# Output projection: the residual rows' loads moved behind the loads of the attention's rows

## The chip, the cores and the metric

One core of one Trainium2 chip. The metric is device time in microseconds (us) of one launch. The engines are TensorE (PE; its weight loads are PEld), VectorE (DVE), ScalarE (ACT), GpSimd (POOL) and SyncE (SP), which here issues every DMA.

## The reference, cut to what matters

Two layers on x (1024 rows, 1024 features). The first mixes windowed attention and a two-way gated delta rule, and projects both back onto the residual:

```python
def first_block(x, ...):
    h = x
    xn = _rmsnorm(h, norm_mix_w[l])
    proj = xn @ w_in[l]
    ...
    attn = _windowed_gqa(q_a, k_a, v_a, band_bias, in_window, attn_sink[l])
    gdn = _gdn_mixer(qkv_g, z_g, a_g, b_g, ...)
    h = h + jnp.concatenate([attn, gdn], axis=-1) @ w_out[l]
    hn = _rmsnorm(h, norm_ffn_w[l])
    h = h + jnp.square(jax.nn.relu(hn @ w_ffn_in[l])) @ w_ffn_out[l]
```

The change bears on the line with `w_out`, and there on how `h` (the residual, the input x) reaches the core's memory. A second layer follows (pooling, convolution and stick-breaking attention, gates, projection); the change doesn't name it.

## The kernel before, in words

Data lies feature-major: 8 row blocks of 128 features by 1024 positions, in two halves of 512 (half 0 and half 1). Every large product is made of three passes over operands split into a high and a low part: high weight by high data (line 631), low weight by high data (633), high weight by low data (635). A product of the output projection, stage P3, is one output block m for one half: 8 row blocks, so 24 matmuls. TensorE takes the products in a fixed order: (m 0, half 1), (1, 1), (0, 0), (1, 0), then m 2 to 4 with both halves each (half 0 first), then m 5 to 7 of half 0, then of half 1.

**Operands of P3.** Row blocks 0 to 3 are the attention's output. Attention runs over 8 blocks of 128 positions; after block n VectorE takes it from its bank (`ao`, line 1648) and, for n under 7, SyncE stores it to DRAM (`aout`, "outgoing rows"). `ya(h, j)` loads row block j of half h back ("the attention's rows"): for half 1 once `aout(6)` is complete, for half 0 once `yah(1, j)` and `yal(1, j)` have read its buffer. `yah` (ScalarE, line 997) makes the high part and `yal` (VectorE, line 1425) the low part. Row blocks 4 to 7 are the delta rule's output: `zl(h, j)` loads gate rows, `zm` (VectorE, 1659) multiplies, `zh` (ScalarE, 997) and `zlo` (GpSimd, 2089) split.

**The residual.** `hx(g, h)` loads row blocks 2g and 2g+1 of half h of x into `H`, 512 KB; there are eight. It may start once `sc` (g 0, 1) or `cR` (g 2, 3) of both directions' last chunk are done (lines 2422 to 2424). Its only reader is `evd` (line 1674), which adds a finished product to its block of `H`: the first four need `hx(0, 1)` and `hx(0, 0)`. Before P3 the norm of the delta rule runs on ScalarE (the square `gsq`, line 1187; `gr`, lines 1001 and 1003) and VectorE (`gn`, line 1608). While P3 runs, VectorE and ScalarE also prepare the next stage: squares and their sums (`hsq`, 1232; `hac`, 1414 and 1416) and splits of feed-forward weights (`ws`).

**What sets the order.** Each engine runs its steps in a fixed order, with semaphore waits. The order is written by a planner (`Plan.settle`): every step has an engine, a cost, its needs and a rank. Again and again it takes, over the engines, the step that can start earliest; among the steps of one engine that could start at the same moment the lowest rank goes first, then the one added first. A step with `behind` isn't offered before the named steps of its own engine are taken. Loads share one modelled transfer line of 330 bytes per ns, so moving a load also moves when the planner sees later loads arrive. SyncE's queue is strictly in order: a step that waits holds up all behind it. Ranks: `wload` (weight tiles, out of in_wo here) 2, `zl` and `ya` 4 less 1.9 for half 1, with 2 more for (0, 3) and 1 more for (1, 2), `hx` 6 less h. The steps are added at lines 3029 to 3039:

```python
        for j in range(4):
            add("sp", "zl", h, j, rank=4 - 1.9 * h + MIX_RANK.get((h, j), 0))
            add("sp", "ya", h, j, rank=4 - 1.9 * h + MIX_RANK.get((h, j), 0))
...
        for g in range(4):
            add("sp", "hx", g, h, rank=6 - h)
```

Of the kernel before, what the change touches and what calls it, by code (L numbers as in the profile page):

```python
# [187 lines left out]
class Plan:  # L188
# [15 lines left out]
    def add(self, engine, name, *key, rank=5, ring=None, frees=None, behind=()):  # L204


        self.steps.append((engine, name, key, rank, ring, frees, behind))
# [2680 lines left out]
def first_layer(p, K):  # L2888

    B = K.bulk  # L2890
    add = p.add
# [137 lines left out]
    for h in range(2):  # L3029
# [3 lines that stand above are left out]
            add("dve", "zm", h, j, rank=4 - 1.9 * h + MIX_RANK.get((h, j), 0))  # L3033
            add("act", "zh", h, j, rank=4 - 1.9 * h + MIX_RANK.get((h, j), 0))
            add("pool", "zlo", h, j, rank=4 - 1.9 * h + MIX_RANK.get((h, j), 0))
            add("act", "yah", h, j, rank=4 - 1.9 * h + MIX_RANK.get((h, j), 0))
            add("dve", "yal", h, j, rank=4 - 1.9 * h + MIX_RANK.get((h, j), 0))
        for g in range(4):
            add("sp", "hx", g, h, rank=6 - h)
    add("dve", "gg")  # L3040
    add("act", "gq")
    for h in range(2):
# [172 lines left out]
def build(nc, A, out):  # L3215
# [12 lines left out]
    for b, j in enumerate(B.jobs):  # L3228
# [14 lines left out]
        else:  # L3243
            p.add("dve", "evd", b, rank=1)
    first_layer(p, K)
    second_layer(p, K)

# [151 lines left out]
```

## Time and profile before

| | us |
|---|---|
| Median of 3 runs | 2312.79 |
| The three runs | 2305.86, 2313.30, 2312.79 |
| The profiled execution | 2304.95 |
| Its span | 2302.9 |

The profile is of one execution. A row of a timeline has its start, its duration, the engine, the line of the kernel, the operation, what it writes and reads, and how many instructions are merged in it; in brackets stands how long the engine had been idle before it and what released it. A line can be that of a helper: DMA issues all have line 2198, copies on ScalarE 997, low parts on VectorE 1425. Matmuls are pipelined, so their rows overlap a little.

### The profile page before, as it was taken

Reading aid. Unit: us, or ns where it says so; the run is one execution under the profiler, and the core shown is the slowest. Engines: PE = TensorE matmul, PEld = TensorE weight load, DVE = VectorE, ACT = ScalarE, POOL = GpSimd, SP = SyncE. Lnnn points to the kernel's source line nnn. Section 1 sums busy time; section 2 is a strip of 40 time slices with the busy share of each in tenths; the row PEclk is TensorE's granted clock in tenths of the full one; section 3 lists DMA queues with packets and bytes.
Section 4 is the critical chain, followed back from the end, with each engine's and each line's share of the span. In section 5 each row is a group of like instructions: output and inputs, shape, how many; then the busy total and the mean of one; then the engine's idle time right before and its main releaser. Section 6 shows DMA issues by size and latency. Waiting matters only on the chain.

```text
span 2302.9 us, 31262 instructions
## 1 busy us (share of the span) xinstructions
PE 2248.1 (98%) x11389; PEld 1780.0 (77%) x11389; DVE 1599.7 (69%) x2217; ACT 1111.1 (48%) x2008; POOL 1034.9 (45%) x643
## 2 busy tenths in 40 slices
PE   9999989899989999999999999999999999999999
PEld 6778867666868888887887777777787888888886
DVE  7865767776597555689539789878978665546745
ACT  5654156765265555544446455655513322225653
POOL 2212245434247766657857211111114775556663
PEclk9999999999999999999999999999999999999999
DMA  4113353335325543855452311111123343338554
GB/s 159 44 40 99 127 175 104 104 111 173 101 74 191 178 149 136 291 180 167 149 174 79 123 37 46 38 47 46 39 95 133 124 138 120 112 120 301 184 173 147
DMA packets 153764, 289.43 MB, mean 126 GB/s; under 512 B 34915, under 2 KB 44387, under 8 KB 153612
## 3 DMA queue, kind: packets, MB, share of 16 engines
q1 hardware_dynamic: 153612, 287.44, 38.0%
q8 instruction: 91, 1.49, 0.3%
q14 instruction: 61, 0.50, 0.1%
HBM read 207.88 MB, written 79.51 MB: 125 GB/s over the span
## 4 chain that ended last, share of the span: by engine, by line
PE 84%; DVE 7%; issue 3%; DMA 3%; ACT 2%; POOL 1%; SPq 0%; DVEq 0%; ACTq 0%; POOLq 0%
PE bank L631 12%; PE bank L635 12%; PE bank L633 12%; PE bank L863 11%; PE bank L861 11%; PE bank L859 11%; PE bank L708 2%; PE bank L924 2%; PE bank L955 2%; PE bank L937 1%; DVE t L1425 1%; ACT t L997 1%; DMA t<-in_wf 1%; PE bank L846 1%; PE bank L836 1%
## 5 line engine op out<-in xcount | busy, mean ns | idle before, releaser
L2089 POOL TENSOR_TENSOR t<-t,t 128x512 fp32r<-128x512 f32 (+1 forms) x494 | 814.8, 1661 | 1065.2 <-ACT t L997 1055.1
L997 ACT ACTIVATE t<-t 128x512 fp32r<-128x512 f32 (+1 forms) x689 | 448.8, 676 | 669.0 <-PE bank L863 258.2
L631 PE MATMUL bank<-t,t 128*128 128x512 f32 x1360 | 549.0, 404 | 0.8 <-ACT t L997 0.8
L635 PE MATMUL bank<-t,t 128*128 128x512 f32 x1360 | 531.6, 391 | 1.8 <-DVE t L1425 1.2
L633 PE MATMUL bank<-t,t 128*128 128x512 f32 x1360 | 529.9, 390 | 1.5 <-POOL t L2089 1.5
L859 PE MATMUL bank<-t,t 128*128 128x512 f32 x1316 | 514.0, 391 | 9.9 <-DVE t L1809 8.4
L863 PE MATMUL bank<-t,t 128*128 128x512 f32 x1316 | 513.3, 390 | 1.6 <-DVE t L1425 1.5
L861 PE MATMUL bank<-t,t 128*128 128x512 f32 x1316 | 513.0, 390 | 0.8 <-POOL t L2089 0.8
L631 PEld LDWEIGHTS bank<-t,t 128*128 128x128 f32 x1360 | 255.6, 188 | 63.7 <-issue 13.1
L635 PEld LDWEIGHTS bank<-t,t 128*128 128x128 f32 x1360 | 255.2, 188 | 60.5 <-DVE t L1425 3.1
L633 PEld LDWEIGHTS bank<-t,t 128*128 128x128 f32 x1360 | 255.8, 188 | 54.8 <-issue 4.6
L859 PEld LDWEIGHTS bank<-t,t 128*128 128x128 f32 x1316 | 247.6, 188 | 63.0 <-DVE t L1809 8.8
L863 PEld LDWEIGHTS bank<-t,t 128*128 128x128 f32 x1316 | 247.5, 188 | 54.1 <-DVE t L1425 3.4
L861 PEld LDWEIGHTS bank<-t,t 128*128 128x128 f32 x1316 | 247.6, 188 | 53.8 <-POOL t L2089 1.7
L1425 DVE TENSOR_TENSOR t<-t,t 128x512 fp32r<-128x512 f32 x192 | 184.7, 977 | 76.2 <-ACT t L997 75.5
L997 ACT ACTIVATE t<-bank 128x512 f32<-128x512 f32 (+2 forms) x255 | 143.3, 579 | 191.2 <-PE bank L937 48.5
L2039 DVE TENSOR_TENSOR t<-t,bank 128x512 f32<-128x512 f32 x105 | 70.2, 682 | 100.3 <-PE bank L863 99.9
L1965 DVE TENSOR_TENSOR_SCAN t<-t,t 128x512 f32<-128x512 f32 (+3 forms) x96 | 104.7, 1091 | 3.3
L1416 DVE TENSOR_TENSOR t<-t,t 128x512 f32<-128x512 f32 x55 | 74.9, 1362 | 29.8 <-ACT t L1373 16.4
L1443 DVE SCALAR_TENSOR_TENSOR t<-t,t,t 128x1024 f32<-128x1024 f32 x48 | 76.3, 1594 | 14.1 <-ACT t L997 12.9
L1725 DVE TENSOR_TENSOR t<-t,bank 128x512 f32<-128x512 f32 x48 | 32.9, 686 | 60.2 <-PE bank L635 55.3
L2134 POOL TENSOR_TENSOR t<-t,t 128x1536 f32<-128x1536 f32 (+1 forms) x16 | 43.3, 2730 | 46.2 <-DVE t L1637 35.1
(250 smaller groups left out, 2663.8 us busy)
## 6 DMA issues: line engine op xcount, KB each, us to landing
t<-in_w SPq DMA_DIRECT2D x87, 512.0 KB, 3.6
hid_scr<-t SPq DMA_DIRECT2D x112, 256.0 KB, 2.2
t<-hid_scr SPq DMA_DIRECT2D x112, 256.0 KB, 2.8
t<-in_wf SPq DMA_DIRECT2D x80, 256.0 KB, 3.3
t<-in_wf SPq DMA_DIRECT2D x36, 512.0 KB, 4.4
g_scr<-t SPq DMA_DIRECT2D x36, 512.0 KB, 2.9
t<-g_scr SPq DMA_DIRECT2D x72, 256.0 KB, 3.6
t<-in_wo SPq DMA_DIRECT2D x24, 512.0 KB, 3.6
```

The costliest lines, as they stand in the source:

```text
L631: e.matmul(ps[:, :], hi[:, w, :], XH[:, x, hs], start=k == 0, stop=False)
L633: e.matmul(ps[:, :], lo[:, w, :], XH[:, x, hs], start=False, stop=False)
L635: last = e.matmul(ps[:, :], hi[:, w, :], XL[:, x, hs], start=False, stop=k == j.nk - 1)
L859: e.matmul(ps, hi, XH, start=start, stop=False)
L861: e.matmul(ps, lo, XH, start=False, stop=False)
L863: return e.matmul(ps, hi, XL, start=False, stop=stop)
L997: return e.activation(out, in_, ACT.Copy, **kw)
L1416: tt(acc[:, :], acc[:, :], sq[:, :], ALU.add).then_inc(*tick(*name))
L1425: return tt(out, x, high.bitcast(F32), ALU.subtract)
L1443: stt(y[:, :] if j < 4 else dst, raw[:, j:j + S], w, y[:, :], ALU.mult, ALU.add).then_inc(*tick("cv", m))
L1965: e.tensor_tensor_scan(x[:, ::-1], one_c.broadcast_to([128, nk]), m_[:, ::-1], 0.0, ALU.mult, ALU.add).then_inc(*tick("ss", a, i, p_))
L2089: return e.tensor_tensor(out, x, high.bitcast(F32), ALU.subtract)
```

## The change

Every `hx` gets a `behind`. `hx(0, 1)` isn't offered before `aout(6)` is in the order of SyncE; each of the other seven not before `ya(0, 3)` is. Ranks, waits, buffers and sizes stay.

```diff
@@ -3036,7 +3036,7 @@
             add("act", "yah", h, j, rank=4 - 1.9 * h + MIX_RANK.get((h, j), 0))
             add("dve", "yal", h, j, rank=4 - 1.9 * h + MIX_RANK.get((h, j), 0))
         for g in range(4):
-            add("sp", "hx", g, h, rank=6 - h)
+            add("sp", "hx", g, h, rank=6 - h, behind=[("aout", (6,))] if h and not g else [("ya", (0, 3))])
     add("dve", "gg")
     add("act", "gq")
     for h in range(2):
```

## Rows read from the trace of the kernel before

**Rows 1.** The page: span, and busy time of TensorE with its share.

```profile
span 2302.9 us, 31262 instructions
...
PE 2248.1 (98%) x11389; PEld 1780.0 (77%) x11389; DVE 1599.7 (69%) x2217; ACT 1111.1 (48%) x2008; POOL 1034.9 (45%) x643
```

**Rows 2.** Stretches (a:b us): length, busy us by engine, clock, DMA share, GB/s.

```profile
534.80:543.30 8.50, 4.27 (x16) 2.15 (x15) 8.50 (x9) 5.71 (x12) 6.33 (x4) 1.00 0.73 261
543.30:634.00 90.70, 90.70 (x399) 74.63 (x398) 51.53 (x62) 27.45 (x45) 24.34 (x14) 1.00 0.34 113
634.00:665.00 31.00, 23.53 (x102) 18.77 (x100) 30.09 (x36) 19.51 (x34) 18.33 (x12) 0.92 0.02 9
```

**Rows 3.** Waits of TensorE, 480 to 550 us: total us, times, longest.

```profile
PE bank L817 <- ACT t L1187: 3.0, 1, 3.0
PE bank L635 <- DVE t L1425: 1.2, 3, 0.7
```

**Rows 4.** Timeline of SyncE's queue, 480 to 570: start, us, line, out<-in, count.

```profile
483.46 2.18 SPq L2198 DMA_DIRECT2D t<-in_xT  x4
...
514.77 2.02 SPq L2198 DMA_DIRECT2D t<-in_xT  x4
526.38 0.37 SPq L2198 DMA_DIRECT2D attn_scr<-t  x1
528.26 0.34 SPq L2198 DMA_DIRECT2D t<-in_wo  x1
528.67 1.36 SPq L2198 DMA_DIRECT2D t<-attn_scr  x3
...
531.91 0.58 SPq L2198 DMA_DIRECT2D t<-attn_scr  x1
...
542.77 0.38 SPq L2198 DMA_DIRECT2D t<-in_wo  x1
543.25 0.38 SPq L2198 DMA_DIRECT2D t<-attn_scr  x1
543.68 0.42 SPq L2198 DMA_DIRECT2D t<-z_scr  x1
```

**Rows 5.** Finer stretches of the same view as rows 2.

```profile
488.00:492.00 4.00, 3.27 (x39) 1.97 (x36) 3.51 (x11) 0.59 (x1) 0.00 (x0) 1.00 0.95 332
...
514.00:518.00 4.00, 2.85 (x21) 1.80 (x20) 1.40 (x6) 4.00 (x15) 1.71 (x1) 1.00 0.78 245
518.00:522.00 4.00, 4.00 (x29) 2.52 (x28) 1.08 (x2) 3.06 (x6) 2.04 (x2) 1.00 1.02 388
...
536.00:538.00 2.00, 0.00 (x0) 0.00 (x0) 2.00 (x3) 2.00 (x5) 2.00 (x2) 1.00 1.04 403
...
548.00:552.00 4.00, 4.00 (x19) 3.30 (x19) 2.53 (x4) 1.86 (x3) 2.42 (x2) 1.00 0.05 18
```

**Rows 6.** Timelines of VectorE, ScalarE, GpSimd, 537 to 564: ends, [idle before <-releaser].

```profile
537.13 2.85 DVE L1425 TENSOR_TENSOR t<-t,t 128x512 fp32r<-128x512 f32 x1
...
538.61 0.63 ACT L997 ACTIVATE t<-t 128x512 fp32r<-128x512 f32 x1 [0.45 <-DMA t<-attn_scr]
...
542.21 0.68 DVE L1425 TENSOR_TENSOR t<-t,t 128x512 fp32r<-128x512 f32 x1
...
548.74 0.63 ACT L997 ACTIVATE t<-t 128x512 fp32r<-128x512 f32 x1 [1.60 <-DMA t<-attn_scr]
...
549.37 0.69 DVE L1659 TENSOR_TENSOR t<-t,t 128x512 f32<-128x512 f32 x1 [3.42 <-DMA t<-z_scr]
...
550.58 0.69 DVE L1425 TENSOR_TENSOR t<-t,t 128x512 fp32r<-128x512 f32 x1
...
550.81 1.61 POOL L2089 TENSOR_TENSOR t<-t,t 128x512 fp32r<-128x512 f32 x1 [1.58 <-ACT t L997]
...
553.82 0.68 DVE L1425 TENSOR_TENSOR t<-t,t 128x512 fp32r<-128x512 f32 x1
...
563.27 0.69 DVE L1674 TENSOR_TENSOR t<-t,bank 128x512 f32<-128x512 f32 x1 [1.56 <-PE bank L635]
```

## The prediction, made before the changed kernel was run

> **What bounds the kernel now.** I read the page first, for the share of each engine. TensorE is busy for 2248.1 of 2302.9 us [rows 1], so all of its idle time is 54.8 us, and a change of loads can win only from that. Next came the busy time by stretch, to see where that idle time lies near the change. From 534.8 to 543.3 us TensorE is busy for 4.27 of 8.50 us; from 543.3 to 634.0, the whole output projection, it is busy for 90.70 of 90.70; from 634 to 665, the way into the feed-forward part, it is idle again for 7.5 us, with VectorE busy for 30.09 of 31.00 and the DMA share at 0.02 [rows 2]. So the projection itself is bound by TensorE, its entry by something else, and the stretch after it by VectorE, with no load in it.
>
> The waits of TensorE name the something: 3.0 us on ScalarE's square of line 1187 and 1.2 us on VectorE's line 1425, the low part of the attention's rows [rows 3]. No DMA stands among them. Then the queue of SyncE: four residual loads at 483.46, four at 514.77 in 2.02 us (0.5 us each to issue), block 6's outgoing rows at 526.38, the attention's rows of half 1 from 528.67, and ya(0,2) and zl(0,2) last, at 543.25 and 543.68 [rows 4]. Last came the timelines of the other engines [rows 6], for how much room each late load has.
>
> **Part 1: eight loads leave 483.46 and 514.77.** What goes is 4.2 us of issuing and 4 MB of transfer. Behind the first four the queue held one outgoing store, behind the second four nothing until 526.38, 9.6 us after they were issued [rows 4]. While they moved, the DMA engines were full (shares 0.95 and 1.02), yet TensorE was busy for 3.27 of 4.00, 2.85 of 4.00 and 4.00 of 4.00 us [rows 5]. Nothing waited for a load there. I cost this at nothing. The bounds: nothing reads these rows that early, so removing them costs at least 0; it gains at most the idle time of 488 to 492 and 514 to 518, 0.73 + 1.15 = 1.9 us, should full DMA engines slow the other engines' reads and writes.
>
> **Part 2: hx(0,1) behind block 6's outgoing rows.** SyncE is free from 526.75 until the weights at 528.26 [rows 4], because it waits there; the 0.5 us of issuing fits into 1.5. No engine is queued behind SyncE but its own loads. The transfer is 512 KB. At the 388 GB/s of the stretch in which four such loads ran [rows 5] it takes 524288 / 388000 = 1.35 us. It goes ahead of the attention's rows, into a time when the engines become full (403 GB/s at 536 to 538 [rows 5]). The one load that has no room is ya(1,2), issued at 531.91: its copy on ScalarE waited 0.45 us for it and ran at 538.61 to 539.24 [rows 4, 6]. Put 1.35 us later it ends at 540.6. Its low part on VectorE started only at 542.21, behind three others, so 1.6 us are left over. The copies of the other three wait for block 7's output instead, not for their loads. Cost: 0. Bounds: 0 below; above, the low part of ya(1,0), which TensorE waits for, took 2.85 us where the same shape takes 0.68 elsewhere [rows 6]. GpSimd was at work beside it and the DMA engines were full; no row parts the two. If the fullness did it, 1.35 us more of it could cost up to 1.35 us. I take 0, since it is nearest to the rows of 518 to 522, where full DMA engines left TensorE busy throughout.
>
> **Part 3: the other seven behind ya(0,3).** They can go out only after ya(0,3), the load ahead of the weights at 542.77. What follows it now is weights, ya(0,2), zl(0,2) [rows 4]. By rank the planner prefers weights (2), then ya and zl (4), then half 1's residual rows (5), then half 0's (6), but rank decides only among steps that it sees ready at once; where it sees the queue free before ya(0,2) is ready it puts a residual load in. I expect one or two there, and five or six behind zl(0,2). Two delay both late loads by 2 x 1.35 = 2.7 us, one by 1.35.
>
> Against what? The fourth product's residual addition starts at 563.27, right on its end [rows 6]. A matmul takes 90.70 / 399 = 0.227 us [rows 2], a product has 24, so 5.46 us. So the third product, the first that reads half 0, starts near 563.0 - 2 x 5.46 = 552.1, and takes 0.68 us per row block, its low operand last. It wants ya(0,2)'s low part at 552.1 + 2 x 0.68 + 0.45 = 553.9, and has it at 551.27: 2.6 us of room. It wants zl(0,2)'s low part (GpSimd, done at 552.42) at 552.1 + 6 x 0.68 + 0.45 = 556.6: 4.2 us of room. The last low part of half 0, ya(0,3)'s, ends at 554.50 and is wanted at 554.6 [rows 6]: 0.1 us of room. It doesn't hang on a moved load, but on VectorE's order. Today VectorE stands still for 3.42 us before 549.37, for zl(0,2) [rows 6]; the planner will see those rows come later and put other steps there (the product with zl(0,3), splits of the next stage's weights, the first residual addition), which pays for the delay. A delay of 2.7 us against 2.6 and 0.1 of room, with work moved into the hole, makes a stall of 0 to 1.5 us; I take 0.3.
>
> The residual rows themselves: hx(0,1), first needed at 552.1 - 5.46 = 546.6, landed some 15 us before. Half 0's first group is the fourth of the seven, first needed at the end of the third product, 557.5. Ahead of its last byte come four residual loads, one tile of weights and two half-size loads, 6 x 1.35 = 8.1 us from 542.8, and some 2 us to land: near 553. The rest is wanted later, one more every second product or slower. From 548 to 552 the DMA share is 0.05 [rows 5]: that hole takes them. Wait for each: 0.
>
> **Sum.** 0 + 0 + 0.3 = +0.3 us against the profiled execution's own 2304.95 us (span 2302.9 and 2.05 around it): 2305.3. That execution lies 7.8 us under the median of the runs shown, 2312.79; one of the three runs is at 2305.86, two at 2313. The four executions have a mean of 2309.2. A new median can come from either end, so I place it midway between mean and median, 2311.0, and add 0.3: **2311.3 us**. A measurement of this kernel can tell about 0.3%, 6.9 us, from no change.
>
> **A price that the page of DMA states.** The Trainium skill, "DMA: Bandwidth & Descriptors", Specifications, puts what one core draws from HBM at about 358 GB/s. By that an estimate of one residual load is 1.46 us, and of seven 10.3. The rows show 388 and 403 GB/s [rows 5], more than that; the measurement decides, and the sum stands on 1.35.
>
> **Rivals.**
> *Slower: the late rows of half 0 behind all seven.* If the written order puts all seven residual loads between ya(0,3) and ya(0,2), the latter lands 7 x 1.35 = 9.5 us later. Its copy started at 548.74 and would start at 558.2; copy and low part take 0.63 + 0.69, ready at 559.5 where 553.9 is wanted. TensorE then stands for 5.6 us at the third row block of the third product: 2304.95 + 5.6 = 2310.6 on the profiled execution's scale, 2311.0 + 5.6 = 2316.6 on the median's. It decides from the third load put ahead (3 x 1.35 over 2.6 us of room). For it: they are free to go the moment ya(0,3) is out. Against it: weights, ya and zl have the better ranks and follow each other without a gap (542.77, 543.25, 543.68). Chance 0.10.
> By a rule of the Trainium skill ("DMA: Bandwidth & Descriptors", Queues, rings and completion order) the descriptors of one issuing queue are consumed in ring order on each DMA engine, which would make this delay the full one. No row here separates it from a shared rate.
> *Faster: the full DMA engines had slowed the attention's chain.* Then 1.9 us come back from part 1, and the 0.45 us before 538.61 if ya(1,2) finds a freer queue: 2302.6, or 2308.7 on the median's scale. Against it: no wait on a load in that stretch. Chance 0.15.
> *The entry gets longer.* 1.35 us on VectorE's 2.85: 2306.6. Chance 0.10. It is inside what can't be told.
> *No new order in effect:* the loads move, nothing else does, 0. That is within the forecast, whose chance is 0.65.
>
> **How the numbers follow.** None of the cases reaches 0.3% by itself: the forecast, the entry and the faster case stay within it, and the slow one is 0.24%. But the executions shown spread by 8 us, so a median can cross 0.3% from either case: 0.12 faster (the faster case with the lower group of runs, and some of the forecast), 0.09 slower (most of the slow rival), 0.79 within. The range goes from 2303.5 (the lowest execution less most of the 2.3) to 2318.0 (the upper group, 2313.3, and most of the 5.6).
>
> **What would show it.** Right: in the queue of SyncE no load of in_xT at 483 and 514, one within 1 us behind the outgoing rows of block 6, seven between 543 and 548; DMA share near 1 from 548 to 552 instead of 0.05; TensorE still busy for all of the projection but some tenths; its entry's waits still 3.0 and 1.2 us. Wrong: TensorE waiting for VectorE's line 1425 or GpSimd's 2089 around 553 to 557 for over 2 us (the slow rival); a residual addition, line 1674, waiting for a load; TensorE's busy share of 488 to 518 up by over 1 us (the faster one); or a different order of steps far behind the projection that moves the span by more than 3 us, which nothing in these rows lets me price.

## The result, and the profile after

The changed kernel takes 2315.09 us (median of 20 runs, 2311.51 to 2319.35), the kernel before in the same measurements 2311.26 (20 runs, 2305.86 to 2315.56). The ratio is 1.0020, with a 95% interval of 1.0013 to 1.0027: slower by 0.2%, some 4.6 us (the two medians themselves differ by 3.8), where 0.3 us had been forecast. It is within the 0.3% that the prediction named as its limit and within its range, but clear of no change.

The page after, to read beside [rows 1]:

```profile
span 2316.8 us, 31263 instructions
...
PE 2258.9 (98%) x11389; PEld 1785.7 (77%) x11389; DVE 1601.0 (69%) x2217; ACT 1111.0 (48%) x2008; POOL 1034.3 (45%) x643
```

The two spans differ by 13.9 us, three times the 4.6, so profiled executions must not be subtracted whole. Already the attention's end stands 4.46 us later here (the square of line 1187 starts at 542.00, before at 537.54). That isn't the change: the matmuls at 482 us, ahead of the first moved load, already start 4.47 us later, and from 325 to 346.6 us the granted clock was 0.53 in this execution and 0.76 in that of before. Below, times of different executions are compared by their distance from that square, the last step that the entry of the projection waits for.

Where does TensorE wait in the projection now? Its waits from 543 to 640 us (total, times, longest), to read beside [rows 3]:

```profile
PE bank L635 <- DVE t L1425: 3.4, 4, 2.2
PE bank L817 <- ACT t L1187: 3.0, 1, 3.0
```

The 3.0 us at the entry is as before. The wait for VectorE's low parts has grown from 1.2 to 3.4 us, and one new wait of 2.2 us makes the difference. TensorE's own timeline places it (start, duration, line, [idle before <-releaser]):

```profile
556.64 0.39 PE L631 MATMUL bank<-t,t 128*128 128x512 f32 x1
...
558.39 0.50 PE L631 MATMUL bank<-t,t 128*128 128x512 f32 x1 [0.23 <-ACT t L997]
558.72 0.40 PE L633 MATMUL bank<-t,t 128*128 128x512 f32 x1
561.32 0.52 PE L635 MATMUL bank<-t,t 128*128 128x512 f32 x1 [2.20 <-DVE t L1425]
561.65 0.61 PE L631 MATMUL bank<-t,t 128*128 128x512 f32 x1
562.06 0.63 PE L633 MATMUL bank<-t,t 128*128 128x512 f32 x1
...
564.62 0.60 PE L633 MATMUL bank<-t,t 128*128 128x512 f32 x1
565.05 0.41 PE L635 MATMUL bank<-t,t 128*128 128x512 f32 x1
...
566.69 0.39 PE L631 MATMUL bank<-t,t 128*128 128x512 f32 x1
```

The third product starts at 556.64, the fourth at 566.69: 10.05 us for 24 matmuls, where before it took 5.50 (552.13 to 557.63 in the same view). The rows hold two losses, a wait and slower matmuls behind it. One is the stand before 561.32, the low part of row block 2. The other comes behind it: up to then a matmul starts every 0.227 us, from 561.65 to 565.05 every 0.425 us. Finer stretches say why (the last three figures are granted clock, DMA share, GB/s):

```profile
558.00:560.00 2.00, 0.89 (x3) 0.30 (x2) 1.57 (x3) 1.38 (x3) 0.55 (x1) 1.00 1.05 405
560.00:562.00 2.00, 0.68 (x2) 0.61 (x3) 1.86 (x2) 0.00 (x0) 0.72 (x1) 0.91 1.05 387
562.00:564.00 2.00, 2.00 (x6) 1.55 (x5) 0.00 (x0) 0.00 (x0) 0.00 (x0) 0.50 1.07 409
564.00:566.00 2.00, 2.00 (x7) 1.53 (x7) 0.00 (x0) 0.00 (x0) 0.00 (x0) 0.73 0.62 251
566.00:568.00 2.00, 2.00 (x10) 1.66 (x9) 0.69 (x1) 1.05 (x2) 0.00 (x0) 1.00 0.01 4
```

The clock granted falls to 0.50 of 2.4 GHz, the lower of its two levels, and is back at 1.00 from 566. Eight intervals at 0.425 instead of 0.227 cost 1.6 us. The starts fall behind their rhythm by 0.39 at 558.39, 0.10 at 558.72 and 2.37 at 561.32, 2.9 us in all. With small rests that makes the 4.55 us by which the product is longer. That is the size of the result: 4.55 / 2311 = 0.20%. Matched one by one, the same matmuls start 4.46 us later than before ahead of the projection, 9.07 us later behind its third product, and 9.06 us later at 666 us, so nothing else is lost in the projection. The other 4.9 us of the 13.9 come in behind 666 us, 1.6 of them around 1793.9 us, where the clock was at 0.50 for 3.4 us in this execution and at 1.00 before. VectorE, ScalarE, GpSimd and SyncE run the same steps (by line and tile) in the same order as before outside 483 to 562 us, so no other order explains them; with one profiled execution of each kernel they can't be told from the spread between executions.

The queue of SyncE after, beside [rows 4]:

```profile
530.84 0.37 SPq L2198 DMA_DIRECT2D attn_scr<-t  x1
531.25 0.51 SPq L2198 DMA_DIRECT2D t<-in_xT  x1
532.73 0.34 SPq L2198 DMA_DIRECT2D t<-in_wo  x1
...
547.22 0.38 SPq L2198 DMA_DIRECT2D t<-in_wo  x1
547.66 0.94 SPq L2198 DMA_DIRECT2D t<-in_xT  x2
548.69 0.41 SPq L2198 DMA_DIRECT2D t<-z_scr  x1
549.20 0.59 SPq L2198 DMA_DIRECT2D t<-attn_scr  x1
549.84 4.48 SPq L2198 DMA_DIRECT2D t<-in_xT  x5
```

The loads moved as the text of the change says: one residual load right behind block 6's outgoing rows, two ahead of the two late loads, five behind. zl(0,2), at 548.69, has also changed places with ya(0,2), at 549.20. And VectorE, ScalarE and GpSimd around the stall, beside [rows 6]:

```profile
550.52 1.78 DVE L1659 TENSOR_TENSOR t<-t,t 128x512 f32<-128x512 f32 x1
552.23 1.78 DVE L1785 TENSOR_TENSOR t<-t,t 128x512 f32<-128x512 f32 x1
553.94 0.67 DVE L1674 TENSOR_TENSOR t<-t,bank 128x512 f32<-128x512 f32 x1
...
557.18 0.68 DVE L1674 TENSOR_TENSOR t<-t,bank 128x512 f32<-128x512 f32 x1
557.77 0.68 DVE L1659 TENSOR_TENSOR t<-t,t 128x512 f32<-128x512 f32 x1
558.89 0.69 DVE L1416 TENSOR_TENSOR t<-t,t 128x512 f32<-128x512 f32 x1 [0.43 <-ACT t L1232]
559.50 2.37 DVE L1425 TENSOR_TENSOR t<-t,t 128x512 fp32r<-128x512 f32 x2
...
557.70 0.63 ACT L997 ACTIVATE t<-t 128x512 fp32r<-128x512 f32 x1 [2.43 <-DMA t<-attn_scr]
...
559.45 1.26 POOL L2089 TENSOR_TENSOR t<-t,t 128x512 fp32r<-128x512 f32 x1 [4.28 <-ACT t L997]
```

ya(0,2) had landed by 557.70, when ScalarE copied it; its low part on VectorE is the first instruction of the merged row at 559.50. VectorE was then in the second residual addition (557.18), and took zm(0,2) and the second sum of squares (558.89, line 1416, for which it waited 0.43 us) before the low part. Before, that low part had stood right behind the first addition. Moving the loads had made the planner write another order for VectorE.

The low part is slow as well as late. Of the 2.37 us of the merged row the first instruction takes 1.77, where it took 0.69 before: GpSimd had started its split 0.05 us ahead of it, at 559.45. So the wait of 2.20 us is about half the place in the order and half (1.1 us) this neighbour, whom the new order put there: with zm(0,2) just ahead of the low part, GpSimd's split of its product becomes ready at the same time.

### The profile page after: what moved, and what is told of

It reads as the page before. It is cut to its first block, busy times and chain, and to the rows that moved or that the text cites. A ratio compares the mean times of both kernels' runs of the same rounds, so it can differ in the third digit from the quotient of the medians.

```text
span 2316.8 us, 31263 instructions
## 1 busy us (share of the span) xinstructions
PE 2258.9 (98%) x11389; PEld 1785.7 (77%) x11389; DVE 1601.0 (69%) x2217; ACT 1111.0 (48%) x2008; POOL 1034.3 (45%) x643
## 3 DMA queue, kind: packets, MB, share of 16 engines
q8 instruction: 91, 1.49, 0.3%
## 4 chain that ended last, share of the span: by engine, by line
PE 83%; DVE 7%; DMA 3%; issue 3%; ACT 2%; POOL 1%; SPq 0%; DVEq 0%; POOLq 0%; ACTq 0%
PE bank L631 12%; PE bank L635 12%; PE bank L633 12%; PE bank L863 11%; PE bank L861 11%; PE bank L859 11%; PE bank L924 2%; PE bank L708 2%; PE bank L955 2%; PE bank L937 1%; ACT t L997 1%; DVE t L1425 1%; PE bank L846 1%; PE bank L828 1%; DMA t<-in_wf 1%
```

## The experiments

Two theories. **Late load:** the stall is set by when ya(0,2) lands. **Order:** it is set by the order that the planner wrote on VectorE, with the low part of row block 2 behind the second addition. All ratios are against the kernel before, on the same chip. "Third product" is the time from its first matmul's start to the next product's, in the one profiled execution. Each experiment has 5 to 12 runs, against 22 to 31 of the kernel before; only differences beyond the interval count.

| Kernel | Median us | Before | Ratio (95%) | Third product us |
|---|---|---|---|---|
| before, profiled | | | | 5.50 |
| the changed kernel | 2315.09 | 2311.26 | 1.0020 (1.0013 to 1.0027) | 10.05 |
| first_only | 2310.21 | 2308.68 | 1.0001 (0.9992 to 1.0010) | 5.44 |
| seven_last | 2310.37 | 2308.68 | 1.0007 (0.9998 to 1.0016) | 5.59 |
| seven_only | 2314.69 | 2308.68 | 1.0026 (1.0016 to 1.0036) | 10.42 |
| one_ahead | 2314.72 | 2308.68 | 1.0026 (1.0018 to 1.0035) | 10.88 |
| before_new_dve | 2313.53 | 2310.50 | 1.0016 (1.0007 to 1.0024) | 9.47 |
| after_old_dve | 2312.06 | 2310.50 | 1.0004 (0.9995 to 1.0012) | 6.99 |
| four_ahead | 2317.57 | 2310.50 | 1.0039 (1.0025 to 1.0053) | 13.28 |
| seven_ahead | 2321.61 | 2310.50 | 1.0048 (1.0036 to 1.0060) | 13.58 |
| low_before_second | 2311.08 | 2307.14 | 1.0013 (1.0004 to 1.0022) | 7.23 |
| before_gg_later | 2314.42 | 2307.14 | 1.0027 (1.0016 to 1.0038) | 9.60 |
| last_gg_later | 2315.89 | 2307.14 | 1.0029 (1.0017 to 1.0041) | 9.89 |

**first_only**, the first part of the change alone:

```diff
-            add("sp", "hx", g, h, rank=6 - h)
+            add("sp", "hx", g, h, rank=6 - h, behind=[("aout", (6,))] if h and not g else ())
```

> Only hx(0,1) moves behind block 6's outgoing rows; the other seven stay at their old places. Both theories put the cost at the seven: TensorE's waits in the projection as before (3.0 and 1.2 us at its entry, none at the third product), time 0.999 to 1.001 of before. A third theory, that the load ahead of half 1's attention rows costs, would give a longer wait at the entry (over 4.5 us in all) and 1.0006 or more.

TensorE's waits from 530 to 620 us:

```profile
PE bank L817 <- ACT t L1187: 3.0, 1, 3.0
PE bank L635 <- DVE t L1425: 1.2, 3, 0.7
```

The entry waits as before, and the time is the same. The load ahead of half 1's attention rows costs nothing that can be told.

**seven_only**, the second part alone:

```diff
+            add("sp", "hx", g, h, rank=6 - h, behind=() if h and not g else [("ya", (0, 3))])
```

> Only the seven move; the order written has one of them ahead of ya(0,2), and VectorE's order is the changed kernel's around the third product. Order theory (VectorE's low part of row block 2 stands behind the second residual addition and a sum of squares): the full stall, 2.2 us of waiting at line 635 and some 4 us in time, 1.0015 to 1.002. Late-load theory (the stall is set by the landing of ya(0,2)): with one load ahead instead of two it lands 1.35 us earlier, the wait falls to about 1 us and the time to 1.0005 to 1.001.

The ratio, 1.0026, is beyond what either theory gave, and the third product takes 10.42 us. The cost sits in the seven. One load ahead instead of two didn't make it smaller. That alone doesn't decide between the theories, since the text above says nothing of ScalarE, whose order isn't the changed kernel's. The copy of ya(0,2) stands ahead of the first square (line 1232) there, so ScalarE waited 3.43 us for the load, and VectorE 3.26 us for the square, before it came to the low part. TensorE's wait was 2.9 us.

**seven_last**, the seven behind the late rows too:

```diff
+            add("sp", "hx", g, h, rank=6 - h, behind=[("aout", (6,))] if h and not g else [("ya", (0, 2)), ("zl", (0, 2))])
```

> hx(0,1) as in the changed kernel, the seven only behind ya(0,2) and zl(0,2), so none is ahead of the late rows and VectorE's order at the third product is that of before. Both theories: no wait at the third product, time 0.9985 to 1.001 of before. If there is still a stall, the seven that follow ya(0,2) in the queue slow it, and both theories lack that.

No stall: the third product takes 5.59 us. The time is at 1.0007, with an interval that holds no change. The third product explains only 0.1 us of the 0.07%. In the profiled execution the entry was longer too: from the square to the third product 15.36 us for 14.59. TensorE waited 3.0 us there as before, but towards the end of this wait the clock fell to 0.50, for 6.8 us (542.3 to 549.1), while before it stayed at 1.00.

**one_ahead**, one residual load ahead of the late rows, six behind:

```diff
+            add("sp", "hx", g, h, rank=6 - h, behind=[("aout", (6,))] if h and not g else [("ya", (0, 3))] if (g, h) == (1, 1) else [("ya", (0, 2)), ("zl", (0, 2))])
```

> As the changed kernel, but one residual load ahead of zl(0,2) and ya(0,2) instead of two; the orders of VectorE, ScalarE and GpSimd are exactly the changed kernel's. Order theory: the same 2.2 us wait and 1.0015 to 1.002. Late-load theory: ya(0,2) lands 1.35 us earlier, the wait is about 1 us, 1.0005 to 1.001.

One thing in that text was wrong: VectorE's and GpSimd's orders are the changed kernel's, but ScalarE's has the copy of ya(0,2) ahead of the first square (line 1232) instead of behind it, as in seven_only. That shows in the rows of ScalarE and then VectorE:

```profile
553.93 0.63 ACT L997 ACTIVATE t<-t 128x512 fp32r<-128x512 f32 x1 [3.50 <-DMA t<-attn_scr]
554.47 0.61 ACT L1232 ACTIVATE t<-t 128x512 f32<-128x512 f32 x1
...
555.12 0.43 DVE L1414 COPY t<-t 128x512 f32<-128x512 f32 x1 [1.96 <-ACT t L1232]
...
556.66 0.68 DVE L1674 TENSOR_TENSOR t<-t,bank 128x512 f32<-128x512 f32 x1
...
558.65 2.36 DVE L1425 TENSOR_TENSOR t<-t,t 128x512 fp32r<-128x512 f32 x2
```

ya(0,2) was copied 553.93 - 539.46 = 14.47 us after the square of line 1187, in the changed kernel 557.70 - 542.00 = 15.70. It landed 1.2 us earlier and the stall got longer: 3.4 us. The late-load theory falls as the sole cause, and the order theory's 2.2 us were too little as well. ScalarE, waiting for the load, held back the square, and VectorE the sum that needs it (1.96 us idle before 555.12) and with it all that follows, the low part included. A late load costs by what is queued behind it in the order, not only by its own landing.

**before_new_dve**, no load moved, the changed kernel's order written onto VectorE and ScalarE:

```diff
-            add("dve", "zm", h, j, rank=4 - 1.9 * h + MIX_RANK.get((h, j), 0))
+            add("dve", "zm", h, j, rank=4 - 1.9 * h + MIX_RANK.get((h, j), 0), behind=[("evd", (K.bulk.at["h", (3, 1), 1],))] if (h, j) == (0, 2) else ())
...
+ (yah, same line)  behind=[("hsq", (3, 1, 0))] if (h, j) == (0, 2) else ()
+ (yal, same line)  behind=[("hac", (3, 1, 1))] if (h, j) == (0, 2) else ()
```

> The kernel before with every residual load at its old place, but VectorE and ScalarE ordered as in the changed kernel around the third product (zm(0,2) behind the second addition, yal(0,2) behind the second sum of squares). Order theory: the stall is there with no load moved, 1.8 to 2.2 us of waiting at line 635, time 1.001 to 1.002 of before. Late-load theory: ya(0,2) lands early, so no wait and 0.9995 to 1.0005.

TensorE, then VectorE's two low parts (one row) and GpSimd's split:

```profile
559.02 0.50 PE L635 MATMUL bank<-t,t 128*128 128x512 f32 x1 [1.12 <-DVE t L1425]
...
560.72 0.78 PE L635 MATMUL bank<-t,t 128*128 128x512 f32 x1 [0.73 <-DVE t L1425]
...
558.28 2.38 DVE L1425 TENSOR_TENSOR t<-t,t 128x512 fp32r<-128x512 f32 x2
...
558.32 1.79 POOL L2089 TENSOR_TENSOR t<-t,t 128x512 fp32r<-128x512 f32 x1 [3.09 <-ACT t L997]
```

Two waits, 1.12 and 0.73 us, the lower clock behind them (0.66 in 560 to 565), a third product of 9.47 us and a ratio of 1.0016. **The order of VectorE and ScalarE alone, without a single load moved, makes the third product 3.97 us longer, of the changed kernel's 4.55.** The longest wait is 1.12 us and not 2.20 because here row block 2's low part started 0.04 us ahead of GpSimd and took 0.69 us; the low part behind it took 1.78.

**after_old_dve**, the changed kernel with VectorE's low part pulled forward:

```diff
-            add("dve", "zm", h, j, rank=4 - 1.9 * h + MIX_RANK.get((h, j), 0))
+            add("dve", "zm", h, j, rank=4 - 1.9 * h + MIX_RANK.get((h, j), 0), behind=[("yal", (0, 2))] if (h, j) == (0, 3) else ())
```

> The changed kernel's loads, two of them ahead of zl(0,2) and ya(0,2), but zm(0,3) held behind yal(0,2), so that VectorE makes row block 2's low part first and waits for it. Order theory: the wait at row block 2 of the third product falls to 0.7 us or less, but the later row blocks come late and may wait for 1 to 2 us at lines 633 and 635. Late-load theory: the wait at row block 2 stays about 2 us. Time 1.0005 to 1.002 by either; the place of the wait tells them apart.

```profile
556.84 0.50 PE L631 MATMUL bank<-t,t 128*128 128x512 f32 x1 [0.66 <-ACT t L997]
```

With the loads as late as in the changed kernel (ya(0,2) is copied 16.07 us after the square, there 15.70), row block 2 waits for 0.66 us, as the order theory had it, and the third product takes 6.99. The waits of 1 to 2 us at later row blocks didn't come. The load's lateness without the new order costs 1.5 us in the third product. In the time, 1.0004 (expected 1.0005 to 1.002), that can't be told from nothing. The two costs, 3.97 and 1.49, are more than 4.55 together, so they overlap.

**low_before_second**, the changed kernel with the low part back ahead of the second addition: zm(0,2) and yal(0,2) right before the second addition instead of right behind it.

```diff
-            p.add("dve", "evd", b, rank=1)
+            p.add("dve", "evd", b, rank=1, behind=[("yal", (0, 2)), ("zm", (0, 2))] if b == B.at["h", (3, 1), 1] else ())
```

> The changed kernel, loads and their order untouched, but VectorE makes zm(0,2) and yal(0,2) right before the second residual addition instead of right behind it and the second sum of squares. Order theory: ya(0,2) had landed by 557.7 in the changed kernel, so its low part can be ready at about 559.1, when TensorE wants it: the wait of 2.2 us falls under 0.5, time 0.9995 to 1.0006 of before. Late-load theory: the wait stays at 2 us or more, 1.0015 to 1.002.

TensorE's waits, 530 to 620 us, and VectorE's rows of the low parts:

```profile
PE bank L635 <- DVE t L1425: 2.0, 4, 0.7
...
552.91 0.68 DVE L1659 TENSOR_TENSOR t<-t,t 128x512 f32<-128x512 f32 x1
553.98 0.69 DVE L1425 TENSOR_TENSOR t<-t,t 128x512 fp32r<-128x512 f32 x1 [0.40 <-ACT t L997]
554.59 0.68 DVE L1674 TENSOR_TENSOR t<-t,bank 128x512 f32<-128x512 f32 x1
555.19 1.19 DVE L1425 TENSOR_TENSOR t<-t,t 128x512 fp32r<-128x512 f32 x1
```

The longest wait falls from 2.2 to 0.7 us, the clock stays at 1.00, and the product takes 7.23 us for 10.05. What is left stands at the next row block: yal(0,3), 1.19 us long from 555.19, is now behind the second addition. The ratio, 1.0013, is above the expected 0.9995 to 1.0006, though its interval reaches into it; 7.23 - 5.50 = 1.7 us would be 1.0007.

**four_ahead** and **seven_ahead**, more residual loads ahead of the late rows:

```diff
+ (four_ahead, zl and ya)   behind=[("hx", (0, 0))] if (h, j) == (0, 2) else ()
+ (four_ahead, hx)          behind=[("aout", (6,))] if h and not g else [("ya", (0, 3))] if (g, h) in ((1, 1), (2, 1), (3, 1), (0, 0)) else [("ya", (0, 2)), ("zl", (0, 2))]
+ (seven_ahead, zl and ya)  behind=[("hx", (3, 0))] if (h, j) == (0, 2) else ()
```

> As the changed kernel, all orders but SyncE's the same, with four residual loads ahead of zl(0,2) and ya(0,2). Both theories: the load now sets the stall; against the changed kernel ya(0,2) lands 2 x 1.35 = 2.7 us later, less what VectorE's order hides (order theory: about 1 us hidden, wait 3.5 to 4; late-load theory: none, wait 4.9). Time 1.0025 to 1.0035.

> All seven residual loads ahead of zl(0,2) and ya(0,2), the slow rival of the prediction. ya(0,2) lands about 5 x 1.35 = 6.8 us later than in the changed kernel if it had to wait for those ahead only; if the loads behind it already shared its time, it lands less later, 2 to 4 us. Wait at row block 2 between 4 and 8 us, time 1.003 to 1.005 of before.

```profile
556.28 0.50 PE L631 MATMUL bank<-t,t 128*128 128x512 f32 x1 [2.69 <-ACT t L997]
...
559.21 0.80 PE L635 MATMUL bank<-t,t 128*128 128x512 f32 x1 [2.19 <-DVE t L1425]
```

```profile
562.47 0.80 PE L631 MATMUL bank<-t,t 128*128 128x512 f32 x1 [5.68 <-ACT t L997]
```

Now the load is felt directly: TensorE waits for the high part (line 631, ScalarE's copy). With four ahead, where all orders but SyncE's are the changed kernel's, that wait is 2.69 us, for 0.23 there, and the wait for the low part stays at 2.19: the load's cost comes on top of the order's, 4.9 us in all, which is the late-load theory's sum (the order theory had 3.5 to 4). The ratio, 1.0039, lies above the expected 1.0035, its interval reaches into it. With seven ahead there is one wait of 5.68 us (the prediction's slow rival: 5.6); VectorE's low part stands ahead of the second sum of squares in that kernel's order, and TensorE doesn't wait for it. The ratio of 1.0048 stands for 11 us, twice the rival's price. Of these 8.1 are in the third product and 0.9 in the entry, where the clock was at 0.50 behind the wait of 3.0 us, as in seven_last.

How late ya(0,2) is, as the start of its copy after the square of line 1187: before 548.74 - 537.54 = 11.20 us; first_only 11.79; seven_last 13.21; one_ahead 14.47; the changed kernel 15.70; four_ahead 18.14; seven_ahead 21.99. Each load that changes from behind to ahead costs 1.2 to 1.3 us. But seven_last has none ahead, and is 1.4 us later than first_only, with the seven behind it in the queue as the only difference around it. Against first_only, which has none on either side, the seven of seven_ahead cost 21.99 - 11.79 = 10.20 us, 1.46 each. The 0.6 us between before and first_only go with zl(0,2), which stands ahead of ya(0,2) in the latter.

**Two attempts at something better.** The entry's low part waits on VectorE behind two tiny products of gains (lines 1663 and 1664; the first took 1.26 us at that place). Held back:

```diff
-    add("dve", "gg")
+    add("dve", "gg", behind=[("yal", (1, 2))])
```

> The kernel before, with the two small products of gains (lines 1663 and 1664, 128x8) held behind yal(1,2), out of the way of the low part of half 1's first row block. They took 1.3 us ahead of it, with TensorE waiting. If that chain sets the entry, the entry gets 0.5 to 1.1 us shorter, time 0.9995 to 1.0000 of before; if the square of line 1187 sets it, nothing changes.

> Both edits: the seven residual loads behind ya(0,2) and zl(0,2), and the gains' products held back. No wait at the third product, entry as in the run with the kernel before: 0.9990 to 1.0005 of before. Nothing says that it beats the kernel before with the gains' products alone.

Both missed, on the slow side, by a low part placed too late on VectorE, as in the change. In the run with the kernel before:

```profile
PE bank L635 <- DVE t L1425: 2.3, 1, 2.3
...
557.79 0.68 DVE L1796 TENSOR_TENSOR t<-t,t 128x512 f32<-128x512 f32 x1
558.40 0.68 DVE L1798 TENSOR_TENSOR t<-t,t 128x512 f32<-128x512 f32 x1
559.00 0.68 DVE L1425 TENSOR_TENSOR t<-t,t 128x512 fp32r<-128x512 f32 x1
```

The planner wrote another order again: yal(0,3), at 559.00, behind two splits of feed-forward weights (lines 1796 and 1798), a wait of 2.3 us in the third product, lower clock behind it, 9.60 us. In last_gg_later the same place has a wait of 2.7 us. What the edit was meant for is small: in last_gg_later the third product starts 14.45 us after the square, before 14.59; in before_gg_later it is 15.34, with the clock at 0.50 in the entry. No kernel here beats the one before.

## Why the prediction was right or wrong

The place was right, the low part of ya(0,2) in the third product; the mechanism was half right. The prediction asked how late the load comes and took the planner's new order as help. The new order was the larger cost. The size, 0.3 us, was off by more than ten times.

- *Part 1, eight loads leave their old places: 0.* Stands. No run with them gone is faster, and in the changed kernel the same matmuls start 4.44 us later than before at 450 us and 4.46 at 538: the stretch that lost the eight loads became no shorter. The faster rival (chance 0.15) didn't happen.
- *Part 2, hx(0,1): 0, bounds 0 to 1.35.* Stands by first_only. The open question of the bound, whether full DMA engines or GpSimd stretch VectorE's instructions, is answered by two sets of rows. In the changed kernel at 557.18 and 557.77, with the DMA share at 1.06 (557 to 558.4) and GpSimd idle, they take 0.68 us. In before_new_dve at 554.00, beside GpSimd (553.75, 1.48 us) and with the DMA share at 0.00 (554 to 555.7), one takes 1.78. GpSimd beside them is enough, full DMA engines are not. The 2.85 us of ya(1,0)'s low part are GpSimd's as well: it started at 537.13, 0.06 us behind a split of 2.36 us, and ended 0.55 us after it.
- *Part 3, one or two loads ahead: right, two.* Their price, 1.35 us each, was near (1.2 to 1.3). That ya(0,2) would come 2.7 us later was too little, it was 15.70 - 11.20 = 4.5: 1.4 for the loads behind it and 0.6 for the exchange with zl(0,2) had been counted as nothing.
- **The step that failed** is "work moved into the hole pays for the delay: a stall of 0 to 1.5 us; I take 0.3". The sentence before it named the very steps that would move (zm(0,3), the splits, the first addition), and the prediction didn't follow them to the end of the line. They filled the hole of 3.42 us and more: from 550.52 to 558.45 VectorE worked without a pause. The low part of row block 2 (rank 4) was put not only behind them but also behind the second addition (rank 1), which can't start before the second product ends, and the second sum of squares, and it ran beside GpSimd. In place of a stall of 0.3 us the runs show a third product 4.55 us longer. The order of VectorE and ScalarE makes 3.97 of that without a moved load (before_new_dve), the late load without the order 1.5 (after_old_dve).
- *The prices that the Trainium skill states.* A load ahead instead of behind made ya(0,2) 1.22 to 1.28 us later, so nearly its full transfer of 1.35 us, as the rule of ring order has it (the Trainium skill, "DMA: Bandwidth & Descriptors", Queues, rings and completion order); by that rule alone the loads behind would have cost nothing, and the 1.4 us between first_only and seven_last speak against that. By the 358 GB/s from HBM that the Trainium skill gives (the same page, Specifications) a load is an estimated 1.46 us. As a rate the traces show more, 409 GB/s at 562 to 564 in the changed kernel, and the measurement decides; as the delay per load, the seven of seven_ahead against none in first_only cost just that, 1.46 us each. So a price by the rate of a full stretch was a little low.
- *The clock was in no term.* The slower matmuls behind the stall cost 1.6 us, more than half of the wait itself. [Rows 2] had shown 0.92 over the stretch with the long stand before the feed-forward part.
- *The slow rival* (all seven ahead, 5.6 us of waiting) had its wait right when run, 5.68, in part by luck: ya(0,2) came 21.99 - 11.20 = 10.8 us later and not 9.5, and the third product, too, began 0.9 us later, by the clock in the entry. Its time was half right: 8.1 us in the product.
- The range held (2315.09 in 2303.5 to 2318.0), but by luck: it reached that far up for the slow rival, which isn't what happened.

## What to carry to other kernels

Where a planner writes the order, a moved load changes when the planner sees its data arrive, and it will reorder engines that the change doesn't name. Before pricing the loads, follow each step that loses its place: look which step of weak rank now stands behind one that waits for the bottleneck engine, and what runs on GpSimd beside it. And price a stand of TensorE in the middle of a product with the slower clock that can follow it: here 2.9 us of waiting became 4.55. It doesn't always follow: the wait of 3.0 us at the entry was followed by the lower clock in four of the thirteen profiled executions and not in the other nine.

## What the runs showed of the hardware that was not expected

- A wait of 2.20 us in a stream of matmuls was followed by the lower clock for 3.4 us, and so were two waits of 1.12 and 0.73 us (before_new_dve); the longer ones of four_ahead and seven_ahead by 6.8 us of it. Waits of 0.66 and 0.7 us (after_old_dve, low_before_second) were followed by none. The length of the wait doesn't settle it: behind the 3.0 us at the entry the clock stayed at 1.00 in nine profiled executions (before and the changed kernel among them) and stood at 0.50 for 3.4 or 6.8 us in four (seven_last, after_old_dve, seven_ahead, before_gg_later).
- Loads queued behind one on the same queue made it later: 13.21 against 11.79 us, with seven of 512 KB behind it and none ahead. One profiled execution of each stands behind this.
- A 128x512 operation of VectorE on two tiles took 0.68 us, beside full DMA engines too. Where it started while a split of GpSimd was running, it ended 0.55 us behind that split, however long it still ran: 537.13 + 2.85 against 537.07 + 2.36 (before), 559.50 + 1.77 against 559.45 + 1.26 (the changed kernel), 555.19 + 1.19 against 554.55 + 1.28 (low_before_second). So a few hundredths of a microsecond decided who was slow: where the low part of row block 2 started first, by 0.03 or 0.04 us (before_new_dve, seven_only, one_ahead), it took 0.68 or 0.69 us and GpSimd's split 1.78 or 1.79 instead of 1.26. The residual addition, which reads a bank, took 0.67 us while GpSimd was at work (553.94 in the changed kernel).
